# Loading each weight tile by quarters instead of halves in a one-core decoder step

## What is computed

```python
h = rmsnorm(x, g)
q, k, v, glu, gate_a, gate_c = split(h @ w_in)           # w_in 2048 x 9216
attn = stick_breaking(q, k, v)                           # prompt, and 8 samples on a paged cache
conv = silu(layernorm(depthwise_conv31(glu)))
x = x + (sigmoid(gate_a) * (attn @ w_pa) + sigmoid(gate_c) * (conv @ w_pc)) @ w_o
h = rmsnorm(x, g_ffn)                                    # then PEER: 16384 experts
s = (h @ w_query) against sub_keys; idx, gate = top 16 of 128 x 128 pairs, in each of 8 heads
act = gelu(h @ expert_u[idx].T)
x = x + (gate * act) @ expert_v[idx]
y = rmsnorm(x, g_final)
```

## Time and profile before

| | us |
|---|---|
| median of 3 runs | 2353.25 (2352.96 to 2355.39) |
| the profiled execution, its own time | 2352.88 |
| its span, first to last instruction | 2351.3 |
| PE busy | 2280.7 (97%) |
| DVE busy | 1775.7 (76%) |
| ACT busy | 1371.0 (58%) |
| share of time in which PE's clock was granted in full | 0.989 |
| DMA, mean over the span | 212 GB/s |

### The profile page before, as it was taken

The page is one execution under the profiler, slowest core; times in us unless marked ns, Lnnn a source line. Parts: engine busy times, 40 slices in busy tenths (PEclk is TensorE's granted clock), DMA queues, the critical chain, the costliest instruction groups (busy, mean ns, idle before and its releaser), DMA issues.

```text
span 2351.3 us, 55305 instructions
## 1 busy us (share of the span) xinstructions
PE 2280.7 (97%) x16868; PEld 2188.5 (93%) x16868; DVE 1775.7 (76%) x3360; ACT 1371.0 (58%) x2525; POOL 292.4 (12%) x354
## 2 busy tenths in 40 slices
PE   8999999999999999999999999999999999899996
PEld 7999989999999999999999999999999888799995
DVE  7775598887766667777778888886788887677776
ACT  6445455557554456666667777775555555455553
POOL 0321100002010000000000000002511121311110
PEclk9999999999999999999999999999999999999998
DMA  6887534446556456566566555556888897677773
GB/s 220 289 292 250 192 129 161 137 132 210 179 180 198 151 172 203 180 192 199 183 184 212 185 192 187 185 190 224 277 300 298 294 317 249 211 243 254 247 251 128
DMA packets 158366, 498.45 MB, mean 212 GB/s; under 512 B 20272, under 2 KB 43192, under 8 KB 158144
## 3 DMA queue, kind: packets, MB, share of 16 engines
q1 hardware_dynamic: 136096, 425.46, 56.4%
q0 software_dynamic: 22176, 71.89, 7.9%
HBM read 472.10 MB, written 25.11 MB: 211 GB/s over the span
## 4 chain that ended last, share of the span: by engine, by line
PE 54%; DVE 3%; issue 3%; DMA 3%; ACT 1%; POOL 1%; DVEq 0%; SPq 0%; PEld 0%; ACTq 0%; PEldq 0%; POOLq 0%
PE ps L2002 15%; PE ps L305 10%; PE ps L302 10%; PE ps L301 10%; PE ps L2006 8%; DMA raw<-expert_v 2%; PE ps L1977 1%; ACT hi L284 1%; DVE lo L289 0%; DVE whl L1855 0%; POOL fin L1591 0%; POOL fin_r L347 0%; DVE x L1955 0%; DVE gacc L1861 0%; PE ps L2020 0%
## 5 line engine op out<-in xcount | busy, mean ns | idle before, releaser
L289 DVE TENSOR_TENSOR lo<-raw,hi 128x512 fp32r<-128x512 f32 x1504 | 1023.1, 694 | 393.6 <-ACT hi L284 333.0
L284 ACT CAST hi<-raw 128x512 fp32r<-128x512 f32 x1504 | 915.3, 618 | 525.9 <-PE ps L305 372.5
L301 PE MATMUL ps<-h_hi,hi 128*128 128x264 f32 (+1 forms) x3200 | 825.1, 287 | 3.7 <-DVE h_lo L878 2.0
L302 PE MATMUL ps<-h_lo,hi 128*128 128x264 f32 (+1 forms) x3200 | 822.2, 286 | 0.0
L301 PEld LDWEIGHTS ps<-h_hi,hi 128*128 128x128 f32 x3200 | 604.6, 189 | 11.8 <-issue 8.9
L302 PEld LDWEIGHTS ps<-h_lo,hi 128*128 128x128 f32 x3200 | 604.6, 189 | 0.4 <-issue 0.2
L2002 PE MATMUL ps<-whl,hi 128*128 128x464 f32 x2048 | 521.9, 376 | 20.3 <-DVE whl L1855 16.5
L305 PE MATMUL ps<-h_hi,lo 128*128 128x264 f32 (+1 forms) x3200 | 525.9, 286 | 14.5 <-DVE lo L289 14.5
L305 PEld LDWEIGHTS ps<-h_hi,lo 128*128 128x128 f32 x3200 | 446.3, 189 | 16.6 <-DVE lo L289 16.6
L2002 PEld LDWEIGHTS ps<-whl,hi 128*128 128x128 f32 x2048 | 349.4, 191 | 48.7 <-issue 22.0
L2006 PEld LDWEIGHTS ps<-whl,lo 128*128 128x128 f32 x2048 | 308.3, 191 | 22.7
(11 more groups left out here) (284 smaller groups left out, 2040.7 us busy)
## 6 DMA issues: line engine op xcount, KB each, us to landing
raw<-u_tiles SPq DMA_DIRECT2D x256, 512.0 KB, 3.8
raw<-expert_v SPq DMA_DIRECT2D x256, 512.0 KB, 5.8
raw<-weights SPq DMA_DIRECT2D x240, 512.0 KB, 3.6
u_spill<-ust POOLq DMA_DIRECT2D x128, 132.0 KB, 2.9
urg<-u_spill SPq DMA_DIRECT2D x32, 464.0 KB, 6.6
qb<-q_spill POOLq DMA_DIRECT2D x8, 512.0 KB, 6.0
x<-xT SPq DMA_DIRECT2D x4, 560.0 KB, 6.7
kvT<-qkv SPq DMA_DIRECT2D x1, 2240.0 KB, 12.2
```

The lines of the kernel that those rows point to most:

```text
L284: nc.scalar.copy(hi[k % SPLIT][:], raw_quarter(k)).then_inc(hi_done, 1)
L289: nc.vector.tensor_tensor(lo[k % SPLIT][:], raw_quarter(k), hi[k % SPLIT][:].bitcast(F32), ALU.subtract).then_inc(lo_done, 1)
L301: pe.matmul(out, a, rhs[0][:, first + j, 0:n], start=start and j == 0, stop=False)
L302: pe.matmul(out, a, rhs[1][:, first + j, 0:n], start=False, stop=False)
```

## The change

`load_half` now issues two transfers instead of one, of 4 blocks each (256 KB, 2 KB in each partition). The one for quarter r waits only until quarter r of the half that was in the slot has been split. Each slot has two semaphores, `raw_in[s][0]` and `raw_in[s][1]`, and `split_hi` waits for its own quarter's. The first four halves are loaded by two transfers each as well.

```diff
-    raw_in = [sem(f"raw_in{s}") for s in range(RAW)]
+    raw_in = [[sem(f"raw_in{s}_{r}") for r in range(2)] for s in range(RAW)]
...
     def load_half(sp, c, s, src):
-        sp.wait_ge(hi_done, 2 * c + 2)
-        sp.wait_ge(lo_done, 2 * c + 2)
-        sp.dma_start(raw[:, s].rearrange("p a b -> p (a b)"), src).then_inc(raw_in[s], 16)
+        for r in range(2):
+            sp.wait_ge(hi_done, 2 * c + r + 1)
+            sp.wait_ge(lo_done, 2 * c + r + 1)
+            sp.dma_start(raw[:, s, QT * r:QT * r + QT].rearrange("p a b -> p (a b)"),
+                         src[:, QT * P * r:QT * P * (r + 1)]).then_inc(raw_in[s][r], 16)
...
-        act.wait_ge(raw_in[k // 2 % RAW], 2 * q0 + 16 * (k // (2 * RAW)) + 16)
+        act.wait_ge(raw_in[k // 2 % RAW][k % 2], 2 * q0 + 16 * (k // (2 * RAW)) + 16)
...
-                sp.dma_start(raw[:, c].rearrange("p a b -> p (a b)"), a_halves[c]).then_inc(raw_in[c], 16)
+                for r in range(2):
+                    sp.dma_start(raw[:, c, QT * r:QT * r + QT].rearrange("p a b -> p (a b)"),
+                                 a_halves[c][:, QT * P * r:QT * P * (r + 1)]).then_inc(raw_in[c][r], 16)
```

## The result

| | before | after |
|---|---|---|
| median, us | 2353.25 (5 runs, 2348.95 to 2360.74) | 2339.81 (5 runs, 2336.73 to 2341.76) |
| ratio | 1 | 0.9928, 95% interval 0.991 to 0.9947 |
| profiled execution, us | 2352.88 | 2341.76 |

What follows compares the result with a forecast made beforehand. PE was taken as the bound, losing 14.4 us to late raw loads in expert_v; less 2.4 unrecovered, 12.0 us off 2352.9 gives 2340.9, plus 0.4 for the median: 2341.3 us, range 2337.0 to 2352.0.

Steps and rivals of the forecast that it cites:

- the sum: Whole kernel: 14.4 us lost in the expert_v stage, less 2.4 unrecovered, gives 12.0 us gain, 2341.3 us.
- What bounds the kernel: PE, 97% busy, loses 14.4 us in two expert_v stretches to late raw loads; earlier stages have next to nothing.
- Issue time and size: First quarter's load in expert_v: 2.1 us from earlier issue plus 0.7 from 256 KB less, 2.8 against waits of 2.1.
- Rival D: SP issues both quarters together after the second split, so only size helps: 2347 to 2353 us, chance 0.05.
- The 0.9 us that PE forgives: In expert_v, an ACT wait of some 0.9 us for a load leaves PE's pace whole.
- The reserve of 2.4 us: Of the 14.4 us in expert_v, 2.4 left unrecovered for costlier 2 KB rows and the fullest stretch.
- rival B: 2 KB rows are dear and fill the DMA in the first pass: slower, mostly 2358 to 2380 us, chance 0.06.
- Rival A: DVE's fixed order, not the load, delays whl in the first pass; only the second gains: 2349 us, chance 0.14.
- C: Each transfer of raw has a large fixed cost, so quarters come one after another: +830 us, chance 0.01.
- The start: First loads: pieces of x issued up to 1.3 us later, costing 0 to +0.4 us, taken as 0.
- Added issues: SP issues 752 more transfers at 0.43 us each, under 40% full, so they are hidden.
- The signs: Expert_v: ACT waits below 10, 1450 or more matmuls, first-pass landings about 5 us, DMA share within 0.03 of 0.90.

Runs made afterwards that it cites:

- size_only: The changed kernel, but both quarters of a half are issued together, only after both have been split; separate transfers and semaphores stay: 2333.94 us, ratio 0.9905.
- early_both: The changed kernel with its early issue, but ACT's cast of a first quarter also waits for the second quarter's transfer: 2339.92 us, ratio 0.9934.
- early_whole: The kernel before with whole halves, but DVE does a half's second split ahead of the gathered block, so the load is issued sooner: 2334.83 us, ratio 0.9914.
- small_gather: The kernel before with gathered rows cut from 4 KB to 512 bytes, gathered experts left out of the result: 2336.54 us, ratio 0.9922.
- expert_only: The changed kernel with quarters only in the stage of expert_v; weights, u_tiles and the first four halves load whole: 2337.68 us, ratio 0.9926.
- start_order: The changed kernel with first quarters issued between the pieces of x, one quarter, not two, between two pieces: 2337.05 us, ratio 0.9924.
- late_both: Both quarters issued together after both splits, unlike the changed kernel, and ACT's first cast also waits for both transfers: 2353.71 us, ratio 0.9984.
- eighths: The changed kernel with each quarter loaded by two 128 KB transfers: 2397.82 us on a slower chip, where the changed kernel takes 2377.01; ratio to before 1.0017.

## Where the prediction held, and where it failed

**The step that failed** is the sum. Its one term, the stage of `expert_v`, stood at 14.4 - 2.4 = 12.0 us and measured 17.2 us. It was too small in two places: 2.4 us were held back as unrecovered, and all of the two stretches came back; and what the stage holds outside these stretches was put at nothing without a reason, where 2.6 us came. By the ratio the changed kernel stands at 0.9928 x 2353.25 = 2336.3 us, against a forecast of 2341.3 and a lower end of the range of 2337.0; the median of its five runs, 2339.81, lies inside the range. The mechanism, loads that come late for ACT and are paid by PE, was right; how much of the change it needs was not.

**What bounds the kernel** held in full. 14.4 us were counted in two stretches, and 14.6 came back there. That the waits of the two first stages had nothing to give held as well (6048 matmuls from 850 to 1600 us, 6040 before).

**Issue time and size.** The prediction added 2.1 and 0.7 us and took them as needed together: the waits go since 2.8 exceeds 2.1. They do go, but either alone is enough: size in size_only, issue in early_both. The half behind the gathered block shows why, the one that is issued at 1892.55 us in the earlier trace rows; these are medians over the 20 or 21 such halves that are cast between 1730 and 1945 us:

| kernel | issue to landing, us | issue to ACT's cast, us |
|---|---|---|
| before | 7.06 | 7.15 |
| early_whole | 6.99 | 7.05 |
| size_only, first quarter | 6.31 | 6.52 |
| small_gather | 6.04 | 6.52 |
| after, first quarter | 5.71 | 7.81 |

At PE's pace and with DVE's order of before, ACT takes this half 6.52 us after its issue, and in before it landed after 7.06. So it was about 0.5 us late, once in four chunks, and 9.0 us over the 22.9 cycles of 235 us are 0.39 us of PE for each. That is all that was to be won there. The smaller transfer brings 7.06 - 6.31 = 0.75 us, so the 0.7 was right; the earlier issue brings 7.81 - 6.52 = 1.3 us and not 2.1, which was read from a cycle that ran late itself. Each is more than 0.5. The medians of all landings in the stretch can't price the size: they are 5.1 us in after, but 5.6 in expert_only and 5.8 in start_order, which load this stage in the same way, against 6.2 before.

**Rival D**, only the size helps, was priced at 2347 to 2353, and that was wrong too: size_only measured 2333.94. The price took "half of the waits below 0.9 us" as half of the gain, and let two transfers compete. In fact all waits fell to 0.7 us or less in the first pass and 1.0 in the second. Had the change done no more than this, its time would have been the same, for another reason.

**The 0.9 us that PE forgives** was read from one wait. Early_whole has waits up to 1.4 us at PE's pace, so 0.9 is a lower bound.

**The reserve of 2.4 us** for dear rows and the fullest stretch was wrong: nothing stayed unrecovered. The engine time, 0.8% more per MB in the first pass and 1.6% more over all, is near the lower end of its range, and the share from 0.90 to 0.94 because the same work is done in less time (0.90 x 1465 / 1407 = 0.937). So **rival B** was far away at this size. **Rival A** is refuted by late_both against size_only: DVE's order is the same in both, and the loads alone decide. **C** was nothing: 4.5 us to land, one each 1.285 us.

**The sum.** 14.4 should have stood in full, and the stretches left out held 17.2 - 14.6 = 2.6 us more, 2.1 of them from 1955 to 2040 us. By the medians the gain is 13.4 us, near the 12.0; by the ratio it is 16.9, near the stage's 17.2, and the forecast's 0.9949 (2341.3 / 2353.25) lies just outside the interval. That the two medians stand only 1.5 us from the forecast is luck in part.

**The start** was taken at 0 with +0.4 as its upper end; it is +0.9, since pieces of `x` do queue behind issues: 1.44 us later for the last of them, with 0.15 us of wait left at ACT and the rest passed down from the second piece. It is lost in the scatter of whole runs.

**Added issues** cost nothing at two a half, as reckoned; but the 0.43 us for one were too few. Eighths shows 0.60 in the loop, and the edge is one doubling away, not beyond reach as "under 40% full" sounds.

**The signs** came as told: waits 0 (below 10), 1465 matmuls (1450 or more), landing 5.1 us (about 5; 5.6 and 5.8 in the two kernels that load alike), share within 0.04 and not 0.03. None of them could tell the theory from its simpler half, size alone. Only an experiment could.

## What to carry to other kernels

Where an engine waits for a ring of loads by 1 or 2 us and the last engine forgives part of it, find first how late the critical load is at the last engine's pace (here 0.5 us), and then the cheapest way to bring that: a semaphore for the part that is used first, an earlier issue, or less traffic beside it all brought the same here, and they don't add up. Price each alone against the margin before adding terms. Split transfers only while the issuing queue still waits for its consumers: here two for 512 KB won 0.7%, and four lost it again.

## What was not expected of the hardware

- Landing time under load depends on the bytes beside a transfer as well as on its own: 512 KB land in 6.1 us beside 4 KB gather rows and in 5.2 us beside 512-byte ones, and 256 KB in 5.1 to 5.6 us. The Trainium skill (DMA: Bandwidth & Descriptors, section "Rules for kernel authors") asks for 1 MiB or more for the most bandwidth. None of the loads changed here has that size. In this case 256 KB with semaphores of their own beat 512 KB by 0.7%, for the latency and not for bandwidth (late_both, with the same transfers, gains next to nothing), and 128 KB lost again, with SP issuing without a pause and the DMA share at 0.91.
- The granted clock's short losses differ from execution to execution (0.90, 0.91, 0.95 and 1.00 over the first 32 us in four of them) and go with a shift of the profiled stage by some 6 us. Two profiles of this kernel are compared by stages, not by their spans.
- Single packets show the price of short rows better than sums do: 4 KB took 159 ns, two of 2 KB 2 x 84 = 168 ns and four of 1 KB 4 x 46 = 184 ns (the medians of the packet records in the traces of before, after and eighths).
- One chip stalled by some 38 us during small gathers that cost nothing visible on the others.
